# Token rows fetched from memory for all pairs of experts but the first, and two experts, not four, combined on the chip

## The chip, the cores and the metric

One core of a Trainium2 chip runs the whole program. The metric is the device time of one execution in microseconds, less is better. The kernel before took 1516.45 us in the median of three runs (1516.04 to 1519.44).

## What is computed

Two layers of a small diffusion trunk over 384 tokens of width 1024 (128 context tokens and 256 sample tokens, three tiles of 128). Layer 0 mixes by differential attention, layer 1 by retention; behind each mixer stands a mixture of experts (MoE), which is what matters here. Everything is float32.

```python
def group_moe(h, w_router, router_bias, w_gate, w_up, w_down):
    t = h.reshape(B * N, D)
    s = jax.nn.sigmoid((t @ w_router).astype(F32))
    ...            # the best of 4 groups, in it the best 2 of 4 experts
    w = w / jnp.sum(w, axis=-1, keepdims=True)
    gates = jnp.sum(jax.nn.one_hot(idx, N_EXPERTS, dtype=F32) * w[..., None], axis=1)

    def expert(y, p):
        wg, wu, wd, ge = p
        a = jax.nn.silu(t @ wg) * (t @ wu) * ge[:, None].astype(t.dtype)
        return y + a @ wd, None
```

16 experts, each with a gate and an up matrix of 1024 x 512 and a down matrix of 512 x 1024. A token uses two of them, so an expert has 48 tokens on average.

## The kernel before

The program is one instruction stream for each engine, written out by hand and tied by semaphores. PE does all matmuls, SP issues all loads of weights, ACT and DVE empty PSUM, POOL (GpSimd) issues indirect DMAs. `plan_jobs` numbers the PSUM banks' jobs in PE's order, `plan_units` the weights' loads.

**The MoE stage** (`experts(l)`, once a layer) turns the normalised activations into token rows `htok` (three tiles of 128 tokens x 1024), in two halves of 512 columns (L924, L1726). The router runs on DVE meanwhile. Then the experts come in pairs (q = 0 to 7, x = 0 or 1, e = 2q + x). For a block of 64 slots of each expert:

1. `gather` (L938, matmul L943): `htok` times a one-hot selection `sel` gives the two experts' tokens, features on partitions, in PSUM banks 2 and 3: 8 feature tiles x 3 token tiles = 24 matmuls a pair (48 instructions, since a float32 matmul is two). ACT copies them to `xs` (L1389), which is double-buffered.
2. gate and up matmuls (L1052, L1053), side by side in two halves of the array, 8 steps of 2 instructions each.
3. SiLU on ACT (L1418), times up on DVE (L1910), four transposes on PE (L1066), a copy by ACT (L1421), the down matmuls (L1083, L1084), a copy to `ysb` by DVE (L1916).

The gather of pair q + 1 stands in the work of pair q: for x = 0 bank 2, for x = 1 bank 3, three feature tiles between the gate matmuls and the wait for the product (L1062), the fourth between L1066 and the down matmuls (L1078). Tokens over 64 of an expert go through blocks of 32 in a loop of its own (`overflow`); in this run's data these are experts 5 and 6 of layer 0 and 4 to 7 of layer 1.

**The results.** `LAST` is 12. Experts 0 to 11 store their rows in HBM (`scratch`, traced as expert_rows, L1430). When expert 11's are stored, POOL reads two rows a token back with six indirect DMAs (L2053); ACT and DVE weigh and add them to `ytok` at the end of expert 13's iteration (L1439, L1920). Experts 12 to 15 are combined on the chip: the slot weights are turned (L1074), `combine` (L1017) multiplies the output by them, DVE adds the result to the residual xT (L1842, or L1583 for expert 15, the last). `side_plan` puts the combines of expert e - 1 in pairs behind odd gate steps of expert e, and the turning of `ytok` (L1032) behind L1074 of expert 14 and even steps of expert 15.

**The weights.** A unit is one 2 MB matrix. Nine places hold them (six in `ring`, three in pieces of other tiles, free only for experts 0 to 11). SP reloads a place when PE has passed L1066 (gate, up) or the down matmuls of the expert before in that place (L594); gate and up of expert 14 and 15 thus wait for L1066 of expert 12 and 13. The rows of expert e wait on ACT, POOL's read-back behind all stores.

Of the kernel before, what the change touches and what calls it, by code (L numbers as in the profile page):

```python
# [16 lines left out]
P = 128  # L17
D = 1024
# [16 lines left out]
LAST = NE - EPG  # L35


def side_plan():

    pair = lambda e, i: [("comb", e, i, 4), ("comb", e, i + 4, 7)]  # L40
    turn = lambda i: [("turn", None, i, 2), ("turn", None, i + 1, 3)]
# [16 lines left out]
WHOLE = 3 * LAST  # L58
# [5 lines left out]
def shape_constants():  # L64

    def angles(width):
# [13 lines left out]
        "first16": np.broadcast_to(np.arange(NE, 0, -1, dtype=np.float32), (P, NE)),  # L80
        "row0": np.broadcast_to(np.arange(NE, dtype=np.float32) * BLK, (P, NE)),
# [152 lines left out]
def trunk_kernel(nc, ins, outs, scratch):  # L234
# [31 lines left out]
    with ctx:  # L266
# [115 lines left out]
        def roT(f):  # L382
# [3 lines left out]
        wm = carve({"htok": TT * D, "xs": 2 * D, "sel": TT * P, "sg": 2 * 512, "aT": 2 * 256,  # L386
                    "y": 2 * 512, "osel": TT * OVB, "ox": KT * OVB, "osg": QC, "oa": QC, "oaT": 2 * BLK, "oy": QC,
                    "yg": TT * D, "selw": TT * P, "wT": TOK, "late": 2 * TOK, "G": TT * EPG, "G2": TT * EPG, "notl": TT, "dg": D, "s": TT * NE, "selb": TT * NE, "pair": TT * NG * 6, "gs": TT * NG,
                    "gm": TT, "gw": TT * NG, "gx": TT, "ing": TT * NG, "pen": TT * NG, "mx": TT, "w": TT * NE,
# [4 lines left out]
        xs = wm["xs"].rearrange("p (n k s) -> p n k s", n=2, k=KT)  # L394
        sel = wm["sel"].rearrange("p (t x s) -> p t x s", t=TT, x=2)
        sg = wm["sg"].rearrange("p (x f) -> p x f", x=2)
# [59 lines left out]
        for l in range(DEPTH):  # L456
# [4 lines left out]
                "o_stored", "picked", "half", "ytok", "passed", "side", "side_added", "selw", "selT", "wT",  # L461
                "o_selT", "o_wT", "o_comb", "o_added")})
# [160 lines left out]
        def _(pe):  # L623
# [292 lines left out]
            def experts(l):  # L916
# [97 lines left out]
                def combine(e, kt, out):  # L1014

                    rows = slice(BLK * (kt // 4), BLK * (kt // 4) + BLK)
                    return mm(out, ysb[rows, e % 2, P * (kt % 4):P * (kt % 4) + P], wT[rows, :], start=True, stop=True)  # L1017

                def side_work(at):

                    for kind, e, kt, place, n, before_, _ in side.get(at, ()):
                        if before_:
                            pe.wait_ge(m["side_added"], before_)
                        if kind == "comb":
                            pe.wait_ge(m["y"], e + 3)
                            pe.wait_ge(m["wT"], e - LAST + 1)
                            last = combine(e, kt, psum[:, place, 0:TOK])
                        else:
                            pe.wait_ge(m["xs"], NE)
                            pe.wait_ge(m["ytok"], TT)  # L1030
                            for t in range(TT):
                                last = tr(psum[:, place, P * t:P * t + P], ytok[:, t, P * kt:P * kt + P], ident)  # L1032
                        last.then_inc(m["side"], 1)

                pe.wait_ge(m["sel"], 1)
                for half in range(2):
                    gather(half, range(4 * half, 4 * half + 4)).then_inc(m["gathered"], 1)
                emptied(pe, ("rank", l))
                pe.wait_ge(m["routed"], 1)
                for it in range(NE // 4):  # L1040
                    for par in range(2):
                        q = it * 2 + par
                        for x in range(2):
                            e = q * 2 + x
                            wg, wu = unit(e, 0), unit(e, 1)
                            for kt in range(KT):
# [4 lines left out]
                                xk = xs[:, par, kt, BLK * x:BLK * x + BLK]  # L1051
# [25 lines left out]
                            if more:  # L1077
                                gather(x, (4 * x + 3,)).then_inc(m["gathered"], 1)  # L1078
# [129 lines left out]
        def _(act):  # L1208
# [158 lines left out]
            def experts(l):  # L1367
# [43 lines left out]
                for it in range(NE // 4):  # L1411
                    for par in range(2):
                        q = it * 2 + par
                        for x in range(2):
# [10 lines left out]
                            if q + 1 < NE // 2:  # L1425
                                take_xs(q + 1, 1 - par, x)
# [664 lines left out]
```

## Time and profile before

| | |
|---|---|
| median of three runs | 1516.45 us |
| the profiled execution | 1517.39 us, its span 1515.6 us |
| PE busy | 1405.8 us, 93% |
| DVE, ACT, POOL busy | 464.1, 281.0, 46.5 us |
| gate and up matmuls (L1052, L1053), with a ring place | 177.1 us each, x384, 605 ns |
| gathers (L943) | 107.0 us, x768, 292 ns |
| copies to xs by ACT (L1389) | 19.1 us, x32, 597 ns |
| chain that ended last | PE 86%; DVE 5%; DMA 3% |
| HBM read | 324.96 MB, 226 GB/s over the span |

The span is divided into 40 slices on the page, each digit a share in tenths; MoE stages are slices 9 to 16 and 31 to 39. A row of the timeline has the start, the length, the engine, line and operation, what it writes and reads, how many were merged, and in brackets the engine's idle time before it with what ended it.

### The profile page before, as it was taken

What the parts mean: (1) busy time and instruction counts of PE and PEld (TensorE: products, weight loads), DVE (VectorE), ACT (ScalarE), POOL (GpSimd) and SP (SyncE); (2) the same over time, 40 slices, a digit from 0 to 9 for tenths busy, and PEclk for the clock granted to TensorE, in tenths of its full rate; (3) what the DMA queues carried; (4) which work ended last, traced back from release to release, by engine and by line L of the source; (5) the groups of instructions that cost most, each with busy time, mean ns of one, the idle gap of its engine ahead of it and who ended that gap; (6) DMA issues with size and microseconds to landing.
All of it is one profiled execution on the core that took longest, in us unless ns stands there. A gap on an engine that the chain in (4) does not pass through costs nothing.

```text
span 1515.6 us, 17269 instructions
## 1 busy us (share of the span) xinstructions
PE 1405.8 (93%) x6556; PEld 721.1 (48%) x6556; DVE 464.1 (31%) x1360; ACT 281.0 (19%) x580; POOL 46.5 (3%) x63
## 2 busy tenths in 40 slices
PE   6999999989999998899999999996898998899887
PEld 2456465655444443344544545543555544444333
DVE  3156266342111135420611603405113211111354
ACT  2144245211101011310211202112101100001112
POOL 1001200000000010000100100000000000000100
PEclk9999999989999998999999999998899999999988
DMA  9877678748999999622233332234114897589951
GB/s 355 295 278 257 186 267 298 267 168 304 397 396 353 398 378 337 211 102 77 99 111 106 116 111 82 85 111 139 55 56 167 301 396 290 214 314 397 361 193 43
DMA packets 162100, 343.75 MB, mean 227 GB/s; under 512 B 5801, under 2 KB 23426, under 8 KB 161986
## 3 DMA queue, kind: packets, MB, share of 16 engines
q1 hardware_dynamic: 150320, 319.19, 57.5%
q0 software_dynamic: 2944, 9.65, 2.4%
q10 hardware_dynamic: 8722, 13.32, 2.4%
q8 instruction: 80, 1.31, 0.4%
q14 instruction: 34, 0.28, 0.1%
HBM read 324.96 MB, written 17.17 MB: 226 GB/s over the span
## 4 chain that ended last, share of the span: by engine, by line
PE 86%; DVE 5%; DMA 3%; ACT 2%; issue 2%; SPq 2%; DVEq 0%; ACTq 0%
PE psum L765 19%; PE psum L1052 14%; PE psum L758 11%; PE psum L1083 8%; PE psum L943 7%; PE psum L1176 6%; PE psum L894 3%; PE psum L1161 3%; PE psum L660 2%; PE psum L1017 2%; PE psum L988 2%; DMA ring<-in_da_w_qkv 1%; SPq L562 1%; DMA ring<-in_w_ada 1%; PE psum L1000 1%
## 5 line engine op out<-in xcount | busy, mean ns | idle before, releaser
L765 PE MATMUL psum<-ring,hT 128*128 128x512 f32 x672 | 289.4, 592 | 0.0
L765 PEld LDWEIGHTS psum<-ring,hT 128*128 128x128 f32 x672 | 127.7, 190 | 159.0 <-issue 157.8
L758 PE MATMUL psum<-hT,ring 128*128 128x384 f32 x512 | 172.9, 496 | 6.8 <-DMA ring<-in_da_w_qkv 3.8
L1053 PE MATMUL psum<-ring,work 128*64 128x512 f32 x384 | 177.1, 605 | 0.0
L1052 PE MATMUL psum<-ring,work 128*64 128x512 f32 x384 | 177.1, 605 | 0.0
L758 PEld LDWEIGHTS psum<-hT,ring 128*128 128x128 f32 x512 | 98.6, 194 | 75.7 <-issue 7.7
L943 PE MATMUL psum<-work 128*128 128x128 f32 x768 | 107.0, 292 | 11.9 <-issue 9.9
L943 PEld LDWEIGHTS psum<-work 128*128 128x128 f32 x768 | 95.8, 201 | 34.2 <-issue 30.4
L1052 PEld LDWEIGHTS psum<-ring,work 128*64 128x64 f32 x384 | 51.0, 138 | 106.8 <-issue 106.5
L1083 PE MATMUL psum<-ring,work 128*64 128x512 f32 x192 | 92.7, 628 | 1.6 <-issue 1.5
L1084 PE MATMUL psum<-ring,work 128*64 128x512 f32 x192 | 92.8, 629 | 0.0
L1916 DVE COPY work<-psum 128x512 f32<-128x512 f32 x32 | 22.1, 691 | 196.2 <-PE psum L1084 196.2
L1418 ACT ACTIVATE work<-psum 64x512 f32<-64x512 f32 x32 | 18.8, 588 | 338.9 <-PE psum L1053 338.9
L1910 DVE TENSOR_TENSOR work<-work,psum 64x512 f32<-64x512 f32 x32 | 22.1, 690 | 161.2 <-ACT work L1418 161.0
L1583 DVE SCALAR_TENSOR_TENSOR xT<-psum,mod,xT 128x128 f32<-128x128 f32 x64 | 22.5, 410 | 115.3 <-PE psum L1176 83.7
L1842 DVE SCALAR_TENSOR_TENSOR xT<-psum,mod,xT 128x128 f32<-128x128 f32 (+1 forms) x128 | 44.4, 410 | 29.3 <-PE psum L1017 25.4
L1961 DVE TENSOR_SCALAR work<-psum,work 128x256 f32<-128x256 f32 x4 | 1.9, 484 | 167.1 <-PE psum L1127 167.1
L660 PE MATMUL psum<-ring,cond 128*32 128x512 f32 x384 | 49.1, 634 | 2.2 <-DMA ring<-in_w_ada 2.1
L1053 PEld LDWEIGHTS psum<-ring,work 128*64 128x64 f32 x384 | 51.1, 138 | 0.0
L1083 PEld LDWEIGHTS psum<-ring,work 128*64 128x64 f32 x192 | 25.6, 144 | 49.5 <-issue 47.4
L1176 PE MATMUL psum<-sq,ring 128*128 128x384 f32 x128 | 45.4, 510 | 0.9 <-ACT hT L1448 0.9
L1176 PE MATMUL psum<-hT,ring 128*128 128x384 f32 x128 | 42.6, 486 | 0.0
(324 smaller groups left out, 1664.0 us busy)
## 6 DMA issues: line engine op xcount, KB each, us to landing
ring<-in_w_ada SPq DMA_DIRECT2D x24, 2048.0 KB, 12.7
ring<-in_moe_w_gate SPq DMA_DIRECT2D x24, 2048.0 KB, 13.1
ring<-in_moe_w_up SPq DMA_DIRECT2D x24, 2048.0 KB, 17.6
ring<-in_moe_w_down SPq DMA_DIRECT2D x24, 2048.0 KB, 18.8
ring<-in_da_w_qkv SPq DMA_DIRECT2D x6, 2048.0 KB, 15.7
sq<-in_moe_w_gate SPq DMA_DIRECT2D x8, 1536.0 KB, 12.4
hT<-in_moe_w_up SPq DMA_DIRECT2D x8, 1536.0 KB, 14.9
work<-in_moe_w_down SPq DMA_DIRECT2D x24, 512.0 KB, 11.0
```

Source lines behind the costliest of these rows:

```text
L660: last = mm(b[32 * j:32 * j + 32, :], cond[:, kt, :], w[:, kt, :], start=kt < 4, stop=kt >= 4)
L758: last = mm(b[:, 0:TOK], w[:, kt, col:col + P], hT[:, kt, :], start=kt == 0, stop=kt == KT - 1)
L765: last = mm(b, hT[:, kt, P * t:P * t + P], w[:, kt, :], start=kt == 0, stop=kt == KT - 1)
L894: last = mm(b[:, 0:TOK], w[:, h, P * (ft % 4):P * (ft % 4) + P], oT[:, h, :], start=h == 0, stop=h == HEADS - 1)
L943: last = mm(out, htok[:, t, P * kt:P * kt + P], sel[:, t].rearrange("p x s -> p (x s)"), start=t == 0, stop=t == TT - 1)
L1052: mm(psum[0:BLK, x, :], xk, wg[kt], start=kt == 0, stop=kt == KT - 1)
L1053: last = mm(psum[BLK:P, x, :], xk, wu[kt], start=kt == 0, stop=kt == KT - 1)
L1083: mm(psum[0:BLK, 5 + x, :], eaT[:, x, k, :], wd[k][:, 0:512], start=k == 0, stop=k == 3)
L1084: last = mm(psum[BLK:P, 5 + x, :], eaT[:, x, k, :], wd[k][:, 512:D], start=k == 0, stop=k == 3)
L1161: last = mm(b, a, v, start=n == 0, stop=n == len(terms) - 1)
L1176: last = mm(b[:, 0:TOK], w[:, k, P * (ft % 2):P * (ft % 2) + P], roT(k), start=k == 0, stop=k == 15)
L1842: last = V.scalar_tensor_tensor(out=xT[:, kt, a:z], in0=src[:, a:z], scalar=mod[:, l, 40 + kt, c:c + 1], in1=xT[:, kt, a:z], op0=ALU.mult, ...
```

## The change

- `LAST` becomes 14: experts 12 and 13 store their rows too, the read-back starts when expert 13's are stored, and only 14 and 15 are combined on the chip.
- ACT stores `htok` in HBM (`token_rows`), one DMA for each half.
- For pairs 1 to 7, PE multiplies `sel` by a column of token numbers (`list_tokens`, 3 matmuls of one column), DVE writes the 128 numbers as integers (`token_list`), POOL fetches the 128 rows of 4 KB into `xrow` with one indirect DMA (`row_loads`), PE turns them (`turn_rows`, 4 transposes for each expert of the pair). Pair 0 is gathered as before. `xs` and `xrow` have one buffer each; ACT copies both halves in the second expert's iteration.
- The fourth part of the gather between L1066 and the down matmuls is gone.
- The turning of `ytok` in the middle is gone: at the end PE adds it to the combines of expert 15 in the same banks, as matmuls with the identity.

```diff
-LAST = NE - EPG
+LAST = NE - 2
+ONCHIP = NE - LAST
...
-    plan[(NE - 2, "T")] = turn(0)
-    for i in range(3):
-        plan[(NE - 1, 2 * i)] = turn(2 * i + 2)
...
# PE
+                def list_tokens(q):
+                    pe.wait_ge(m["sel"], q + 1)
+                    if q > 1:
+                        pe.wait_ge(m["listed"], q - 1)
+                    chosen = sel_second if q == 1 else sel
+                    for t in range(TT):
+                        last = mm(psum[:, 4, 0:1], chosen[:, t].rearrange("p x s -> p (x s)"),
+                                  table(base_sb, base_at, "token")[:, t:t + 1], start=t == 0, stop=t == TT - 1)
+                    last.then_inc(m["ids"], 1)
+                def turn_rows(q, half):
+                    pe.wait_ge(m["rows"], 16 * q)
+                    pe.wait_ge(m["xs"], 2 * q)
+                    for kt in range(4 * half, 4 * half + 4):
+                        last = tr(psum[:, 2 + half, P * (kt % 4):P * (kt % 4) + P], xrow[:, P * kt:P * kt + P], ident)
+                    last.then_inc(m["gathered"], 1)
                 pe.wait_ge(m["sel"], 1)
-                for half in range(2):
-                    gather(half, range(4 * half, 4 * half + 4)).then_inc(m["gathered"], 1)
+                gather(0, range(4)).then_inc(m["gathered"], 1)
                 emptied(pe, ("rank", l))
+                list_tokens(1)
+                gather(1, range(4, KT)).then_inc(m["gathered"], 1)
...
                             overflow(e, wg, wu, hint)
                             more = q + 1 < NE // 2
+                            if x == 0 and q + 2 < NE // 2:
+                                list_tokens(q + 2)
                             if more:
-                                pe.wait_ge(m["sel"], q + 2)
-                                pe.wait_ge(m["xs"], q * 2 + x + 1)
-                                gather(x, range(4 * x, 4 * x + 3))
+                                turn_rows(q + 1, x)
                             pe.wait_ge(m["gated"], e + 1)
...
-                            if more:
-                                gather(x, (4 * x + 3,)).then_inc(m["gathered"], 1)
...
                 for ft in range(KT):
-                    b = open_job(("y", l, ft))
-                    done(combine(NE - 1, ft, b[:, 0:TOK]))
+                    combine(NE - 1, ft, early(("y", l, ft))[:, 0:TOK], stop=False)
+                pe.wait_ge(m["ytok"], TT)
+                for ft in range(KT):
+                    b = early(("y", l, ft))
+                    for t in range(TT):
+                        last = mm(b[:, P * t:P * t + P], ytok[:, t, P * ft:P * ft + P], ident, start=False, stop=t == TT - 1)
+                    open_job(("y", l, ft))
+                    done(last)
# ACT
+                for half in range(2):
+                    emptied(act, ("htok", l, TT * half + TT - 1))
+                    act.dma_start(token_rows_d.rearrange("(t p) d -> p t d", p=P)[:, :, 512 * half:512 * half + 512],
+                                  htok[:, :, 512 * half:512 * half + 512]).then_inc(m["kept"], 16)
...
-                            if q + 1 < NE // 2:
-                                take_xs(q + 1, 1 - par, x)
+                            if x and q + 1 < NE // 2:
+                                take_xs(q + 1, 0)
+                                take_xs(q + 1, 1)
# DVE
+                def token_list(q):
+                    dve.wait_ge(m["ids"], q)
+                    V.tensor_copy(ids[:, q:q + 1], psum[:, 4, 0:1]).then_inc(m["listed"], 1)
                 select(0)
+                select(1)
...
                             overflow(e, lo, hint)
+                            if x == 0 and q + 2 < NE // 2:
+                                token_list(q + 2)
# POOL, ahead of pick_rows(l)
+            def row_loads(l):
+                m = M[l]
+                pool.wait_ge(m["kept"], 32)
+                for q in range(1, NE // 2):
+                    pool.wait_ge(m["listed"], q)
+                    if q > 1:
+                        pool.wait_ge(m["gathered"], 2 * q)
+                    pool.indirect_dma_start(out=xrow, out_offset=None, in_=token_rows_d,
+                                            in_offset=bass.IndirectOffsetOnAxis(ap=ids[:, q:q + 1], axis=0)).then_inc(m["rows"], 16)
```

## Rows read from the trace of the kernel before

**Rows 1.** Busy time by stretch: length, engines, PE clock, DMA share, GB/s.

```profile
348.20:538.20 190.00, 182.78 (x1163) 86.91 (x1164) 26.62 (x55) 21.35 (x40) 0.00 (x0) 1.00 0.98 370
538.20:617.50 79.30, 71.44 (x342) 28.27 (x338) 38.81 (x104) 10.15 (x17) 5.72 (x6) 0.94 0.82 304
1182.50:1406.10 223.60, 206.49 (x1535) 99.58 (x1536) 33.77 (x76) 22.39 (x43) 0.00 (x0) 1.00 0.86 321
1406.10:1493.80 87.70, 75.02 (x342) 30.39 (x338) 38.87 (x104) 12.48 (x25) 5.67 (x6) 0.90 0.59 221
...
370.00:442.00 72.00, 69.45 (x467) 33.50 (x467) 10.47 (x22) 7.63 (x15) 0.00 (x0) 1.00 1.04 398
454.00:466.00 12.00, 9.66 (x106) 6.06 (x100) 1.57 (x5) 1.25 (x3) 0.00 (x0) 1.00 0.73 257
```

**Rows 2.** Timeline of expert 0 in layer 0, a plain one.

```profile
348.20 0.64 PE L1052 MATMUL psum<-ring,work 128*64 128x512 f32 x1
...
354.69 0.59 PE L1052 MATMUL psum<-ring,work 128*64 128x512 f32 x1
...
355.22 2.27 PE L943 MATMUL psum<-work 128*128 128x128 f32 x18
...
355.96 0.69 DVE L1910 TENSOR_TENSOR work<-work,psum 64x512 f32<-64x512 f32 x1 [6.46 <-ACT work L1418]
...
357.43 0.46 PE L1066 MATMUL psum<-base_sb,work 64*128 64x64 f32 x4
...
358.68 0.64 PE L1083 MATMUL psum<-ring,work 128*64 128x512 f32 x1
...
362.17 0.59 PE L1052 MATMUL psum<-ring,work 128*64 128x512 f32 x1
```

**Rows 3.** Timeline of experts 14 and 15 in layer 0, around L1066.

```profile
589.52 0.69 DVE L1910 TENSOR_TENSOR work<-work,psum 64x512 f32<-64x512 f32 x1
...
590.36 0.43 PE L1066 MATMUL psum<-base_sb,work 64*128 64x64 f32 x4 [2.36 <-DVE work L1910]
...
613.08 0.43 PE L1066 MATMUL psum<-base_sb,work 64*128 64x64 f32 x4 [2.36 <-DVE work L1910]
...
614.00 0.13 PEld L1083 LDWEIGHTS psum<-ring,work 128*64 128x64 f32 x1 [0.25 <-issue]
```

**Rows 4.** Timeline: transposes of 128x128, and matmuls of one column.

```profile
597.94 0.88 PE L1032 MATMUL psum<-base_sb,sq 128*128 128x128 f32 x6
...
1507.30 0.73 PE L705 MATMUL psum<-base_sb,ssp 128*128 128x1 f32 x6
```

**Rows 5.** Landing times: line L2053, line L1430, then loads issued in 1417 to 1418.

```profile
DMA to landing us min/median/max: 4.6/10.0/12.6
...
DMA to landing us min/median/max: 5.2/5.8/6.9
...
ring<-in_moe_w_up SPq DMA_DIRECT2D x1, 2048.0 KB, 21.9
```

**Rows 6.** Timeline of experts 13 and 14 in layer 0.

```profile
552.37 0.59 PE L1052 MATMUL psum<-ring,work 128*64 128x512 f32 x1
...
566.08 0.46 PE L1066 MATMUL psum<-base_sb,work 64*128 64x64 f32 x4
...
592.90 1.06 PE L1083 MATMUL psum<-ring,work 128*64 128x512 f32 x1
```

**Rows 7.** Loads of expert 15's up unit: issued in 566 to 568, 1440 to 1441.

```profile
ring<-in_moe_w_up SPq DMA_DIRECT2D x1, 2048.0 KB, 19.4
...
ring<-in_moe_w_up SPq DMA_DIRECT2D x1, 2048.0 KB, 15.8
```

**Rows 8.** Timeline: ytok in layer 0, the tail of layer 1.

```profile
572.04 3.68 DVE L1920 SCALAR_TENSOR_TENSOR sq<-hT,work,sq 128x1024 f32<-128x1024 f32 x3
...
1494.83 4.25 PE L1017 MATMUL psum<-work 64*128 64x384 f32 x16 [0.79 <-DVE work L1916]
1495.85 5.29 DVE L1583 SCALAR_TENSOR_TENSOR xT<-psum,mod,xT 128x128 f32<-128x128 f32 x16 [1.07 <-PE psum L1017]
```

More of the change, by code:

```diff
@@ L80, in shape_constants @@
         "first16": np.broadcast_to(np.arange(NE, 0, -1, dtype=np.float32), (P, NE)),
+        "token": (P * np.arange(TT)[None, :] + part[:, None]).astype(np.float32),
         "row0": np.broadcast_to(np.arange(NE, dtype=np.float32) * BLK, (P, NE)),
@@ L393, in trunk_kernel @@
         htok = wm["htok"].rearrange("p (t d) -> p t d", t=TT)
-        xs = wm["xs"].rearrange("p (n k s) -> p n k s", n=2, k=KT)
+        xs = wm["xs"].rearrange("p (k s) -> p k s", k=KT)
         sel = wm["sel"].rearrange("p (t x s) -> p t x s", t=TT, x=2)
+        second = wm["at"]["osg"]
+        sel_second = work[:, second:second + TT * P].rearrange("p (t x s) -> p t x s", t=TT, x=2)
+        ids = wm["ids"].bitcast(mybir.dt.uint32)
+        xrow = wm["xrow"]
         sg = wm["sg"].rearrange("p (x f) -> p x f", x=2)
@@ L461, in trunk_kernel @@
                 "o_stored", "picked", "half", "ytok", "passed", "side", "side_added", "selw", "selT", "wT",
+                "kept", "ids", "listed", "rows",
                 "o_selT", "o_wT", "o_comb", "o_added")})
@@ L1012, in overflow, with combine @@
                                 pe.sem_inc(m["o_comb"], 2)
-                def combine(e, kt, out):
+                def combine(e, kt, out, stop=True):
                     rows = slice(BLK * (kt // 4), BLK * (kt // 4) + BLK)
-                    return mm(out, ysb[rows, e % 2, P * (kt % 4):P * (kt % 4) + P], wT[rows, :], start=True, stop=True)
+                    return mm(out, ysb[rows, e % 2, P * (kt % 4):P * (kt % 4) + P], wT[rows, :], start=True, stop=stop)
                 def side_work(at):
@@ L1023, in side_work @@
                             pe.wait_ge(m["side_added"], before_)
[L1024 to L1032, printed above, removed]
-                        last.then_inc(m["side"], 1)
+                        pe.wait_ge(m["y"], e + 3)
+                        pe.wait_ge(m["wT"], e - LAST + 1)
+                        last = combine(e, kt, psum[:, place, 0:TOK])
+                        last.then_inc(m["side"], 1)
+                def list_tokens(q):
[13 more added lines that the diff above has]
+                    last.then_inc(m["gathered"], 1)
                 pe.wait_ge(m["sel"], 1)
-                for half in range(2):
-                    gather(half, range(4 * half, 4 * half + 4)).then_inc(m["gathered"], 1)
+                gather(0, range(4)).then_inc(m["gathered"], 1)
                 emptied(pe, ("rank", l))
+                list_tokens(1)
+                gather(1, range(4, KT)).then_inc(m["gathered"], 1)
                 pe.wait_ge(m["routed"], 1)
@@ L1385, in experts, with take_xs @@
                 act.sem_inc(m["o_stored"], 64)
-                def take_xs(pair, par, half):
+                def take_xs(pair, half):
                     act.wait_ge(m["gathered"], pair * 2 + half + 1)
-                    A(xs[:, par, 4 * half:4 * half + 4, :].rearrange("p k s -> p (k s)"), psum[:, 2 + half, :], ACT.Copy).then_inc(m["xs"], 1)
+                    A(xs[:, 4 * half:4 * half + 4, :].rearrange("p k s -> p (k s)"), psum[:, 2 + half, :], ACT.Copy).then_inc(m["xs"], 1)
                 def overflow(e, hint):
@@ L2087 @@
     scratch = nc.dram_tensor("expert_rows", ((LAST + MAXOV) * BLK, D), mybir.dt.float32, kind="Internal").ap()
-    trunk_kernel(nc, ins, outs, scratch)
+    token_rows_d = nc.dram_tensor("token_rows", (TOK, D), mybir.dt.float32, kind="Internal").ap()
+    trunk_kernel(nc, ins, outs, scratch, token_rows_d)
     r = run_bass_kernel_spmd(nc, [arrays], core_ids=[0])
```

41 lines of the change are left out of this document (23 added, 18 removed).

## The prediction

> **What bounds the kernel now.** I read the page's 40 slices first, then the stretches of the two mixture-of-experts (MoE) stages, then the timeline of single experts. The change touches only these two stages: experts 0 to 11 of layer 0 run from 348.2 to 538.2, 12 to 15 to 617.5; layer 1 has 1182.5 to 1406.1 and then to 1493.8. In the first stretch PE is busy 183 of 190 us and the 16 DMA engines work at a share of 0.98; in long parts of it they are at 1.04 and 398 GB/s, which is as full as the trace ever shows them [rows 1]. So two resources are close to their ends: PE takes 13.9 us for a plain expert, and its 6.3 MB of weights (three units of 2.097 MB) take about 16.1 us at 390 GB/s. The transfers keep up only because nine units are loaded ahead, and because experts with a second block and the last four experts run slowly. In layer 1 there is more of that slowness, and the DMA share is 0.86, then 0.59 [rows 1]. Layer 0 is thus nearly bound by the weights, layer 1 is bound by PE and its waits.
>
> **Part 1, the gathers become transposes (7 of 8 pairs in each layer).** In a plain expert the first gate matmul is at 348.20 and that of the next expert at 362.17. The last gate matmul starts at 354.69 and is through at 355.12; 18 gather instructions fill 355.22 to 357.43, where the transposes of the gated block (L1066) start; the other 6 of the 24 follow, and the down matmuls start at 358.68 [rows 2]. But these gathers were cover. SiLU and the product (L1910) run beside them; the product starts at 355.96. Where no gather stands, L1066 starts 0.84 us after the product's start (589.52 to 590.36), so here it could start at 356.80 and not at 357.43: about 0.65 us are won. Between L1066 and the down matmuls the bare distance is 0.92 us (613.08 to 614.00) against 1.25 with six gathers [rows 2, 3]: 0.3 us. Instead of about 3.1 us of PE work an expert thus gives back about 0.95 us. The new work fits under the same cover: four transposes are about 0.5 us (six last 0.88, starts 0.12 apart), the token list's six one-column matmuls 0.7 us [rows 4]; together 1.2 of the 1.65 us between the last gate matmul and L1066. An expert goes from 13.9 to 13.0 us on PE. With a second block the cover isn't needed, and about 1.7 us are won. At the start of a stage one list and one more selection (DVE) cost 0.7 us once. Halves 0 and 1 of the next pair are now both copied by ACT behind the second expert's L1066: 1.2 us under 3.4 us of down matmuls, so free; without them, xs would be late by these 1.2 us.
>
> **Part 2, where the rows come from.** ACT issues two stores of 0.79 MB, POOL seven fetches of 128 rows (0.52 MB), one a pair. Queued behind each on POOL are the later fetches and then the read-back of expert rows. A fetch starts when the pair before is turned, and PE waits for it after the next expert's gate matmuls: 0.5 us of turning less, that is 1.1 + 0.95 + 3.45 + 6.9 + 0.7 = 13 us later. The nearest rows are the read-backs of the same size, 4.6 us at least and 12.6 at most (six in a row, the last ones behind the first), and the stores of 128 KB in a full stage, 5.2 to 6.9 us [rows 5]. I take 6 us plus 1 us of POOL, by the first of a row; both ends fit into 13, so the fetch is hidden. The price is in bytes. For the first fetch: the rows are written by about 339, the store of half 1 lands some 8 to 9 us later by these rows, the fetch at 353 to 355, and it's wanted at 355.8. I take 0, with 0 to 3 us for each layer.
>
> As for the arbitration, the row shows that the quickest read-back landed after 4.6 us, while a load of 2 MB issued beside the read-backs at 1417.6 took 21.9 us [rows 5]. The Trainium skill (DMA: Bandwidth & Descriptors, "Queues, rings and completion order") says that every DMA engine takes turns between the queues that have work. By that the fetch doesn't stand behind the weights, and the trace agrees; standing behind them it would be the last rival below.
>
> **Part 3, the last four experts.** Removed per layer: the combines of experts 12 and 13, the slot weights and their three transposes, the read-back rows' turning in the middle, and the stalls around them. In layer 0 24.3 us lie between the L1066 of experts 13 and 14 (566.08, 590.36), because DVE first finishes the read-back rows, PE waits for it, the last time 2.36 us, and the clock falls [rows 3, 6]. Now 12, 13 and 14 take 13.0 us each on PE. Expert 15 keeps eight combines, like 13 before: 552.37 to 566.08 less 0.5 us of cover and then 4.4 us, together 17.6 us [rows 6]. The sum is 56.6 us against 79.3 and 87.7. On PE alone the stages would get shorter by 35 us (12 from the gathers, 0.7 lost, 23 here) and 45 us (14 and 31). That isn't the gain, as the weights don't come that fast.
>
> **Part 4, the weights as the new bound.** Expert 15's up unit is the last that gates PE. In layer 0 it is issued at 567.1 and lands 19.4 us later, at 586.5 [rows 7]. The queue has been nearly full since 357. What comes on top before that point is six fetches (3.1 MB) and the rows of experts 12 and 13 (0.5 MB): 3.7 MB, or 9.4 us at 390 GB/s. Off goes the hole at 454 to 466 (share 0.73, 3.6 us [rows 1]), since PE frees slots earlier. So it lands at about 592.3. Behind it stand 10.9 us of gate and up with combines, 2 us for a half clock after the wait (a down matmul lasted 1.06 instead of 0.59 us after such a wait [rows 6]), 2.3 to L1066, 0.95, and 3.45 of down: 19.6 us. The stage ends at 611.9 instead of 617.5, 5.6 us earlier.
>
> In layer 1 it is issued at 1440.7 and lands at 1456.5 [rows 7]. Now expert 7 frees its slot about 10 us earlier, at 1335 (eight experts: 4 at 0.95 and 4 at 1.7, less 0.7). From there to that unit 17 units, six experts' rows, two or three fetches and the 3.1 MB of read-backs have to pass, 42 MB, so 108 us and 2 of latency: 1445 to 1446. PE would be there at about 1435 and waits 10 us. With the same 19.6 us the stage ends at 1465.4, 28.4 us earlier.
>
> **Part 5, the new tail.** The read-back rows are now added after expert 15. The combines start 0.75 us after the copy of y starts and last 3.9 us to the last issue. Beside them DVE makes ytok (3.68 us behind the 0.69 us copy), and ACT's halves lie under the down matmuls. Then come 48 instructions at 0.12 us, 5.6 us, and a last residual of 0.7 us: 11.1 us from the copy. Before it is 7.1 us (16 residuals end at 1501.1) [rows 8]. Cost: 4.0 us a layer, 8 in all. The read-backs themselves start about 6.5 us after expert 13 and need 19; experts 14 and 15 with their wait last over 40 us, so they are hidden.
>
> **Sum.** -5.6 - 28.4 + 8 = -26 us, and I keep -25.5 for what remains of the sequencer's stalls in layer 1. The profiled execution took 1517.39 us (span 1515.6) and would take 1492; it is 0.06% over the median of 1516.45, so the forecast of the median is 1491 us.
>
> **The rivals.**
>
> Rival A, the transfers give more. With 397 GB/s held throughout (the full stretches show 398) the unit of expert 15 lands some 6 us earlier in layer 0 and 3 in layer 1: 1481 us. For it speaks [rows 1], against it that read-backs and weights together came to 389.
>
> Rival B, a slower clock. Every expert now has two short waits on PE, some 1.1 and 0.5 us. After three of the four waits of 2.36 us the granted clock was down at the next down matmuls. If it falls to 1.2 GHz in every expert for about four matmul pairs, each costs 1.7 us, and a plain expert 14.7 us, 0.8 more than before. Layer 0 stays on its weights (-5), layer 1 gets slower by 7 (-21): 1498 to 1500 us. Against it: the waits are half as long, and transposes stand in them. The Trainium skill (TensorE: Matmul & The Clock Gate, "What's actually happening") has idle time as what throttles and sustained work as what releases; [rows 6] agree for the long waits, no row shows the short ones.
>
> Rival C, on the other side: the fetches come late. If a fetch stands behind queued weights like a load of 2 MB, it lands after 22 us and not 7, and PE idles 9 us at each of six pairs in each layer. That takes 54 us where PE alone would have gained 35 and 45: +19, +9 and the tail's 8, so 1552 us. It decides from a landing time of about 19 us (6 us late a pair, where 36 eats the gain). Against it are [rows 5].
>
> Rival D, it does nothing to the time: with one DMA resource full in both layers and clock and first fetch each at their bad end (3 us each, 2 more in each wait), the gain of layer 1 shrinks to the tail's price: 1514 us. Little speaks for all of this together.
>
> **How the numbers follow.** Forecast 0.60 (1484 to 1500 for it alone), A 0.12, B 0.13, C 0.09, D 0.06. The range goes from below A (bandwidth and stalls both kind, 1476) to above B (first fetch late, 1508) and leaves C, D and a bit of A out. Within 0.2%, 1513.4 to 1519.5, is what a measurement of this kernel can't tell from no change; that is D for the most part, 0.05. Faster: 0.60 + 0.12 + 0.13 less a bad end of B = 0.83. Slower 0.12.
>
> **What would show it right or wrong.** Plain experts of 13.0 us, with L1066 about 1.65 us after the gate matmuls. PE waits for DMA on the ring before the gate matmuls of experts 12 to 15, longest (about 10 us) before 15. DMA share over 1.0 up to about 590 in layer 0. The layer-0 stage shorter by 1 to 3 us with its tail, layer 1 by some 24. POOL's fetches landing in 5 to 8 us. Wrong would be: waits for xrow before the turning, a granted clock of 0.5 inside plain experts, or ytok as the last releaser at the tail by several us.

## The result, and the profile after

The changed kernel takes 1506.04 us (median of 4 runs, 1504.49 to 1507.36), the kernel before 1516.24 beside it (1515.92 to 1519.44). The ratio is 0.9921, 95% interval 0.9904 to 0.9937: 10 us faster, 0.8%. 25.5 us were forecast. The profiled execution took 1504.49 us, its span is 1502.6; that is 13.0 less than the span of before, 1515.6.

The first rows are busy time by stretch of the changed kernel: experts 0 to 11 and 12 to 15 of layer 0, the same of layer 1, and the middle of layer 0 once more (columns as in [rows 1]).

```profile
347.00:529.60 182.60, 161.41 (x959) 69.45 (x959) 29.96 (x76) 20.17 (x40) 5.91 (x7) 0.98 1.02 388
529.60:611.70 82.10, 59.67 (x238) 21.38 (x237) 15.18 (x40) 8.96 (x15) 5.62 (x6) 0.81 0.93 349
1180.80:1402.70 221.90, 188.85 (x1329) 82.55 (x1330) 36.91 (x96) 21.30 (x43) 6.61 (x7) 0.96 0.88 334
1402.70:1475.50 72.80, 53.77 (x240) 19.81 (x236) 15.21 (x40) 11.23 (x23) 5.63 (x6) 0.91 0.79 303
400.00:587.00 187.00, 152.59 (x886) 64.30 (x883) 28.53 (x68) 16.83 (x35) 9.37 (x10) 0.93 1.04 397
```

Beside [rows 1] the four stretches went from 190.0, 79.3, 223.6 and 87.7 us to 182.6, 82.1, 221.9 and 72.8. The last four experts of layer 0 got longer, though PE works 12 us less in them (59.7 instead of 71.4), and the first twelve of layer 1 are hardly shorter, though PE works 17.6 us less in them. The last row holds the reason for layer 0: 187 us at a DMA share of 1.04 and 397 GB/s, as full as the fullest row of [rows 1] and without its hole.

Next, what PE waited for in each stage of the changed kernel (us in total, times, longest), layer 0 and then layer 1.

```profile
PE psum L1069 <- DMA ring<-in_moe_w_up: 13.1, 2, 6.6
PE psum L1098 <- issue: 11.5, 14, 2.7
PE psum L1083 <- DVE work L1946: 8.8, 12, 1.5
PE psum L1083 <- issue: 4.9, 1, 4.9
...
PE psum L1098 <- issue: 13.9, 14, 2.4
PE psum L1083 <- DVE work L1946: 10.0, 11, 2.3
PE psum L1069 <- DMA ring<-in_moe_w_up: 9.4, 1, 9.4
...
PE psum L1069 <- issue: 2.9, 1, 2.9
...
PE psum L1048 <- DMA work<-token_rows,work: 2.0, 1, 2.0
```

In both layers the gate matmuls (L1069) now wait for weights. The 11.5 and 13.9 us ahead of the down matmuls (L1098) are waits of about 0.5 us, one in each plain expert up to 13, and six of 1.8 to 2.7 us; those stand in the experts with a second block. This is expert 5 of layer 0, from the end of its second block on (timeline: start, duration, what it does, in brackets the idle time before and what ended it):

```profile
429.23 0.66 PE L1048 MATMUL psum<-base_sb,work 128*128 128x128 f32 x4
...
429.82 0.46 PE L1083 MATMUL psum<-base_sb,work 64*128 64x64 f32 x4
...
430.10 1.95 ACTq L1430 DMA_DIRECT2D expert_rows<-work  x4
...
432.27 0.38 ACT L1446 ACTIVATE work<-psum 128x256 f32<-128x256 f32 x1 [6.20 <-issue]
...
432.75 1.09 PE L1098 MATMUL psum<-work 128*64 128x512 f32 x1 [2.47 <-issue]
...
433.63 1.06 PE L1098 MATMUL psum<-work 128*64 128x512 f32 x1
```

The turned block is ready at about 430.3, but ACT copies it at 432.27, because its queue first issues the four stores of the second block's rows (1.95 us). PE idles 2.47 us, and then its matmuls last 1.06 to 1.09 us, not 0.59: half clock. Before, the same four issues lay under 18 gathers and the transposes behind them:

```profile
435.09 2.28 PE L943 MATMUL psum<-work 128*128 128x128 f32 x18
...
435.96 1.86 ACTq L1405 DMA_DIRECT2D expert_rows<-work  x4
...
437.30 0.46 PE L1066 MATMUL psum<-base_sb,work 64*128 64x64 f32 x4
...
438.03 0.38 ACT L1421 ACTIVATE work<-psum 128x256 f32<-128x256 f32 x1 [6.09 <-PE psum L1066]
...
438.55 0.64 PE L1083 MATMUL psum<-work 128*64 128x512 f32 x1
```

Last, expert 0 of layer 1 in the changed kernel, where the first fetch comes late, and the landing times of the fetches (L2086) and of the stores of the rows (L1406):

```profile
1190.60 1.11 PE L1048 MATMUL psum<-base_sb,work 128*128 128x128 f32 x4 [1.99 <-DMA work<-token_rows,work]
...
1192.86 1.08 PE L1098 MATMUL psum<-ring,work 128*64 128x512 f32 x1 [0.52 <-issue]
...
DMA to landing us min/median/max: 7.0/8.4/9.2
...
DMA to landing us min/median/max: 7.6/8.0/9.1
```

PE waits 1.99 us ahead of the turning (L1048), then the down matmuls run at half clock, and the expert takes 17.5 us instead of 13.0.

### The profile page after: what moved, and what is told of

Read it like the earlier page. It is cut to its first block, busy times and chain, and to the rows that moved or that the text cites. A ratio compares the mean times of both kernels' runs of the same rounds, so it can differ in the third digit from the quotient of the medians.

```text
span 1502.6 us, 16129 instructions
## 1 busy us (share of the span) xinstructions
PE 1341.8 (89%) x6052; PEld 680.2 (45%) x6052; DVE 428.1 (28%) x1256; ACT 276.4 (18%) x576; POOL 59.6 (4%) x77
## 4 chain that ended last, share of the span: by engine, by line
PE 75%; DMA 11%; DVE 4%; SPq 4%; issue 3%; ACT 3%; DVEq 0%; ACTq 0%; POOLq 0%
PE psum L768 19%; PE psum L761 11%; PE psum L1069 11%; PE psum L1098 6%; PE psum L1197 6%; DMA ring<-in_moe_w_up 5%; PE psum L897 3%; PE psum L1182 3%; SPq L597 2%; PE psum L663 2%; PE psum L991 2%; DMA ring<-in_da_w_qkv 1%; SPq L565 1%; DMA token_rows<-work 1%; DMA work<-token_rows,work 1%
## 5 line engine op out<-in xcount | busy, mean ns | idle before, releaser
L1069 PE MATMUL psum<-ring,work 128*64 128x512 f32 x384 | 178.6, 617 | 25.5 <-DMA ring<-in_moe_w_up 22.5
L1070 PE MATMUL psum<-ring,work 128*64 128x512 f32 x384 | 178.8, 618 | 0.0
L1069 PEld LDWEIGHTS psum<-ring,work 128*64 128x64 f32 x384 | 53.2, 142 | 132.2 <-issue 131.9
L1098 PE MATMUL psum<-ring,work 128*64 128x512 f32 x192 | 96.9, 652 | 17.7 <-issue 17.6
L1099 PE MATMUL psum<-ring,work 128*64 128x512 f32 x192 | 97.5, 656 | 0.0
L1098 PEld LDWEIGHTS psum<-ring,work 128*64 128x64 f32 x192 | 26.6, 149 | 65.0 <-issue 65.0
L1070 PEld LDWEIGHTS psum<-ring,work 128*64 128x64 f32 x384 | 53.1, 142 | 0.0
L663 PE MATMUL psum<-ring,cond 128*32 128x512 f32 x384 | 46.0, 598 | 2.8 <-DMA ring<-in_w_ada 2.7
L1197 PE MATMUL psum<-sq,ring 128*128 128x384 f32 x128 | 45.2, 509 | 0.9 <-ACT hT L1474 0.9
L1069 PE MATMUL psum<-sq,work 128*64 128x512 f32 x96 | 42.5, 592 | 0.0
L1070 PE MATMUL psum<-hT,work 128*64 128x512 f32 x96 | 42.5, 592 | 0.0
L897 PE MATMUL psum<-sq,ring 128*128 128x384 f32 x128 | 42.1, 488 | 0.0
## 6 DMA issues: line engine op xcount, KB each, us to landing
ring<-in_w_ada SPq DMA_DIRECT2D x24, 2048.0 KB, 12.6
ring<-in_moe_w_up SPq DMA_DIRECT2D x24, 2048.0 KB, 19.6
```

Of the source, the lines that this page charges most:

```text
L663: last = mm(b[32 * j:32 * j + 32, :], cond[:, kt, :], w[:, kt, :], start=kt < 4, stop=kt >= 4)
L897: last = mm(b[:, 0:TOK], w[:, h, P * (ft % 4):P * (ft % 4) + P], oT[:, h, :], start=h == 0, stop=h == HEADS - 1)
L1069: mm(psum[0:BLK, x, :], xk, wg[kt], start=kt == 0, stop=kt == KT - 1)
L1070: last = mm(psum[BLK:P, x, :], xk, wu[kt], start=kt == 0, stop=kt == KT - 1)
L1098: mm(psum[0:BLK, 5 + x, :], eaT[:, x, k, :], wd[k][:, 0:512], start=k == 0, stop=k == 3)
L1099: last = mm(psum[BLK:P, 5 + x, :], eaT[:, x, k, :], wd[k][:, 512:D], start=k == 0, stop=k == 3)
```

## The experiments

Theory 1: the missing gain is PE time lost in the experts with a second block and in expert 0 of layer 1, so that slots come free late, and above that the bytes ahead of expert 15's up unit. Theory 2: the transfers alone set both stages, whatever PE does. The table gives for every kernel the four stretches of the profiled execution in us (from first gate matmul to first gate matmul, the last stretch of a layer to the end of expert 15's down matmuls), the median, and its ratio to the kernel before with the interval.

| kernel | L0, 0-11 | L0, 12-15 | L1, 0-11 | L1, 12-15 | us | ratio |
|---|---|---|---|---|---|---|
| before | 190.0 | 79.3 | 223.6 | 87.7 | 1516.2 | 1 |
| changed | 182.6 | 82.1 | 221.9 | 72.8 | 1506.0 | 0.9921 (0.9904-0.9937) |
| k1_one_store | 185.2 | 81.5 | 210.4 | 74.8 | 1498.1 | 0.9873 (0.9853-0.9892) |
| k2_late_turn | 184.1 | 80.0 | 217.6 | 74.7 | 1502.2 | 0.9907 (0.9890-0.9923) |
| k3_no_fetch | 181.9 | 79.0 | 222.1 | 68.0 | 1493.4 | 0.9838 (0.9817-0.9860) |
| k6_both | 184.5 | 80.1 | 212.0 | 78.3 | 1497.5 | 0.9863 (0.9842-0.9884) |
| k4_gather_last14 | 190.8 | 63.2 | 223.5 | 61.7 | 1483.1 | 0.9770 (0.9755-0.9786) |
| k5_fetch_last12 | 184.2 | 92.3 | 217.4 | 81.6 | 1512.4 | 0.9971 (0.9960-0.9982) |
| k8_held | 184.5 | 75.4 | 217.0 | 65.0 | 1491.1 | 0.9831 (0.9813-0.9850) |
| k7_one_store_held | 185.1 | 75.7 | 213.2 | 66.8 | 1483.9 | 0.9780 (0.9767-0.9792) |
| k9_gather_store_held | 188.9 | 61.7 | 225.4 | 63.2 | 1481.1 | 0.9748 (0.9724-0.9771) |
| k10_no_fetch_one_store | 178.4 | 79.0 | 212.3 | 68.3 | 1483.1 | 0.9767 (0.9744-0.9790) |
| k11_all_three | 184.7 | 76.0 | 212.1 | 65.9 | 1483.9 | 0.9772 (0.9749-0.9795) |

The ratio of k1, k2, k3 and k6 is to one set of runs of the kernel before (median 1516.6), that of k4, k5, k7 and k8 to another (1516.9), that of k9, k10 and k11 to a third (1518.2). So a difference of 2 us between medians of different sets tells nothing. A profile is one execution, and in it down matmuls run at half clock in some experts and not in others: a stretch differs by 1.7 us for each such expert.

**One store in place of four.**

```diff
-for j in range(4):
-    act.dma_start(scratch[ds(o * OVB + LAST * BLK, OVB), QC * j:QC * j + QC],
-                  oy[OVB * j:OVB * j + OVB, :]).then_inc(m["o_stored"], 16)
+act.dma_start(scratch[ds(o * OVB + LAST * BLK, OVB), :].rearrange("s (j c) -> j s c", j=4),
+              oy).then_inc(m["o_stored"], 16)
```

The waits that count these transfers are adapted.

> The changed kernel, but the rows of each second block go to memory with one transfer that ACT issues, not with four. Theory 1 (the missing gain of layer 1 sits in the experts with a second block: the gathers used to cover ACT's four transfer issues, 1.95 us, and now the down matmuls wait for ACT's copy and then run at half clock): in these experts the wait ahead of the down matmuls falls from 2.3 to 3.2 us to about 1.2, the down matmuls from about 5 to 3.5 us, so each of the six takes some 22.5 to 24 us (the two-block one 34) instead of 24.3 to 26.9; expert 15's up unit is issued 8 to 11 us earlier in layer 1 and the whole kernel takes 1494 to 1498 us instead of 1506. Theory 2 (the transfers of layer 1 are full and set its end, whatever PE does): the experts get quicker, the wait for the weights ahead of experts 14 and 15 gets longer by the same time, and the kernel stays at 1504 to 1506 us. In layer 0, where both theories have the weights as the bound, 0 to 2 us.

Measured 1498.1 us, 8 less, at the slow end of theory 1's range. The same place in its timeline:

```profile
432.02 1.16 ACTq L1429 DMA_DIRECT2D expert_rows<-work  x1
...
433.39 0.38 ACT L1445 ACTIVATE work<-psum 128x256 f32<-128x256 f32 x1 [5.39 <-issue]
...
433.87 0.61 PE L1098 MATMUL psum<-work 128*64 128x512 f32 x1 [1.67 <-issue]
```

One issue takes 1.16 us where four took 1.95, PE idles 1.67 us, not 2.47, and the clock holds (0.61). The six experts take 23.5, 25.1, 25.1, 34.3, 23.7 and 23.4 us, where the changed kernel had 25.7, 26.9, 26.3, 37.2, 24.3 and 25.9: 11.2 us less, 7.1 of it in layer 1. Two of the six still fell to half clock (25.1 us). The single profile flatters layer 1 by 4.5 us, since its expert 0 happened not to wait for the fetch. Theory 1 holds in layer 1, and theory 2 fails, as the bytes are the same. In layer 0 nothing is gained: the stage is 2 us longer in this profile, and PE waits 10.4 us for the weights ahead of expert 15, where the changed kernel has 6.6.

**The first fetched pair turned later.**

```diff
-if more:
+if more and q:
     turn_rows(q + 1, x)
+if x and q == 0:
+    turn_rows(1, 0)
+    turn_rows(1, 1)
```

> The changed kernel, but both halves of the pair of experts 2 and 3 are turned behind expert 1's gate matmuls, and none behind expert 0's, so the first fetch has 13 us more. Theory 1: expert 0 of layer 1 goes from 17.5 back to 13.0 us (2.0 us of waiting for the fetch, 2.5 us of half clock behind it); expert 1 gains at most 0.3 us for its four more transposes; the kernel takes 1502 to 1503.5 us instead of 1506. Theory 2 (transfers set the end of layer 1): 1505.5 to 1506.5 us, with a wait for the weights that is 4 us longer ahead of experts 14 and 15.

Measured 1502.2 us, 3.8 less by the medians, in theory 1's range. The mechanism fits only in part: expert 0 of layer 1 takes 14.7 us, not the 13.0 of theory 1. The wait for the fetch is gone, but its down matmuls still ran at half clock (5.15 us to the next expert's start, in place of 3.46), in layer 0 too.

**Six fetches left out.**

```diff
 pool.wait_ge(m["listed"], q)
 if q > 1:
-    pool.wait_ge(m["gathered"], 2 * q)
+    continue
```

PE then waits for the first fetch alone.

> The changed kernel with six of the seven fetches of each layer left out: experts 4 to 15 work on the rows that the first fetch brought, so their part of the result isn't the reference's. It takes 3.1 MB a layer off the queues and any wait for these fetches. The forecast priced these bytes at about 8 us ahead of expert 15's up unit in layer 0, so its stage ends 6 to 8 us earlier, and in layer 1, where PE's own time decides when that unit is issued, 1 to 3 us: 1495 to 1499 us. If bandwidth alone sets the end of both stages (theory 2) both give 8 us: about 1490 us. If the fetches cost nothing (the queues have room for them) it stays within 1504 to 1506 us.

Measured 1493.4 us, 12.6 less, more than the forecast's price (1495 to 1499 us) and less than theory 2's (about 1490). Its profiled execution was the slowest of its four (1498.35 us), so the split by stage is only rough: -3.8 in layer 0, -4.6 in layer 1, where expert 15 alone lost 3.7 us, for the most part to half clock (23.3 us, not 19.6). In layer 0 the 3.1 MB are 7.8 us at 397 GB/s; by an estimate 2.0 of them went back because the queue then ran empty for a while, with a share of 0.88 in this stretch,

```profile
453.00:466.00 13.00, 9.78 (x116) 5.33 (x110) 1.72 (x6) 0.76 (x2) 0.00 (x0) 1.00 0.88 314
```

Another 1.9 us, by which expert 0 was longer at half clock (14.9 us, not 13.0), would make up the rest; that this held back the transfers by as much is not shown.

**Both repairs of PE's waits.** The two edits above in one kernel.

> The changed kernel with the one transfer for the rows of a second block and the late turning of the first fetched pair together. Theory 1: both gains add in layer 1, as both bring the issue of expert 15's up unit forward, less what the queues then can't carry (expert 15's unit would wait behind others for 2 to 4 us): 1491 to 1495 us, near the 1491 us that were forecast. Theory 2: 1504 to 1506 us.

Measured 1497.5 us, outside both ranges and not told apart from k1_one_store. The gains don't add: the first twelve experts of layer 1 are 9.9 us shorter than in the changed kernel, but the last four 5.5 us longer. Of these 5.5 us 3.7 are expert 15 itself (23.3 us, not 19.6, with its down matmuls at half clock), in a profiled execution 4 us above the median. Theory 1's sum was too simple here.

**The second half of the change alone.** To the kernel before, gathers kept:

```diff
-LAST = NE - EPG
+LAST = NE - 2
+ONCHIP = NE - LAST
```

with the change's parts that follow from it: the side plan without turning, the mask of two experts, and the tail with the identity.

> The second half of the change alone: the kernel before with its gathers kept, but only experts 14 and 15 combined on the chip and the read-back rows added by the identity in the tail. No rows are stored or fetched (3.7 MB a layer less than in the changed kernel), and the experts with a second block keep the gathers that cover ACT's four transfer issues. Theory 1 (the fetches' bytes and the lost cover took most of what the transposes give): nearly all of the gain is here. Layer 1: experts 12 to 14 at 13.9 us, the weights for 15 about 1449 to 1453, its stage ends at about 1471 instead of 1493.8; layer 0: up unit at 584 to 587, stage end 604 to 611; two tails of 4 us; together 1490 to 1498 us, faster than the changed kernel's 1506. Rival (the transposes in place of the gathers carry the gain, as PE bounds both layers): 1504 to 1512 us.

Measured 1483.1 us: 34 us faster than before, 23 faster than the whole change, beyond what was expected. Busy time by stretch, same four as above:

```profile
348.90:539.70 190.80, 182.84 (x1163) 86.90 (x1164) 26.63 (x55) 21.35 (x40) 0.00 (x0) 1.00 0.98 370
539.70:602.90 63.20, 59.36 (x280) 23.61 (x276) 15.68 (x41) 9.17 (x15) 5.73 (x6) 0.92 1.02 383
1171.00:1394.50 223.50, 206.29 (x1533) 99.47 (x1534) 33.79 (x76) 22.37 (x43) 0.00 (x0) 1.00 0.87 323
1394.50:1456.20 61.70, 56.67 (x280) 22.90 (x276) 15.70 (x41) 11.50 (x23) 5.67 (x6) 0.97 0.81 309
```

The first twelve experts are as before, and the last four are 16.1 and 26.0 us shorter. Ahead of no expert does PE wait for weights. With experts of 13.9 us the transfers just keep up; with 13.0 us and the fetches' bytes on top they don't.

**The first half of the change alone.** The changed kernel with the old split:

```diff
-LAST = NE - 2
+LAST = NE - EPG
```

and the turning of the read-back rows back in the side plan, the combines of expert 15 closing the tail by themselves.

> The first half of the change alone: rows kept in memory, fetched and turned for seven of eight pairs, but the last four experts combined on the chip and the read-back rows turned beside them, as before. Theory 1: eight plain experts a layer give 0.95 us each on PE, second-block experts give nothing or lose 1 to 2 us each, the first fetch of layer 1 costs up to 4.5 us, and in layer 0 the 3.1 MB of fetches delay expert 15's up unit by up to 5 us: 1512 to 1519 us, no gain that can be told. Rival (the forecast's own terms, 0.95 and 1.7 us for each expert with nothing against them in layer 1): layer 1 gives 12 us, layer 0 loses up to 5: 1504 to 1510 us.

Measured 1512.4 us, 4.5 less than before (0.3%), at the good end of theory 1's range and outside the rival's. It wins 5.8 and 6.2 us in the first twelve experts of the two layers and 6.1 in the last four of layer 1, and loses 13.0 in the last four of layer 0, where PE waits 10.9 us for weights ahead of expert 13. Halves of 34 and 4.5 us together give 10: the first half takes away much of what the second half brings.

**The read-backs held until the last up unit has landed.**

```diff
+unit_wait(pool, ("moe", l, 3 * (NE - 1) + 1))
 settle(pool, l)
 idx = wm["idx"].bitcast(mybir.dt.uint32).rearrange("p (c t) -> p c t", c=2)
```

> The changed kernel, but POOL issues the six read-backs of expert rows (3.1 MB) only when expert 15's up unit has landed, not 8 to 12 us before. Theory 1 (the bytes that lie in the queues ahead of that unit set when the last expert starts; the read-backs' 3.1 MB are 7.8 us of it at 397 GB/s): expert 15's gates start at 579 to 582 us instead of 586.7 in layer 0 and at 1448 to 1450 instead of 1456.1 in layer 1, and the rows are still in time for the tail (they need 14 us, the tail comes 25 us later): 1490 to 1496 us. Rival (a 2 MB unit needs its 15 to 30 us whatever else is queued, or the rows then come too late for the tail): the start of expert 15 moves by less than 2 us or the tail waits for ytok by what was won: 1504 to 1508 us.

Measured 1491.1 us, 15 less. The start of expert 15 in layer 1, first in the changed kernel, then in this one:

```profile
1425.27 8.21 SPq L597 DMA_DIRECT2D ring<-in_moe_w_up  x1
...
1437.10 0.94 POOL L2102 DMA_INDIRECT work<-expert_rows,work  x1 [37.98 <-DMA expert_rows<-work]
...
1456.06 1.09 PE L1069 MATMUL psum<-ring,work 128*64 128x512 f32 x1 [9.41 <-DMA ring<-in_moe_w_up]
```

```profile
1419.47 8.50 SPq L597 DMA_DIRECT2D ring<-in_moe_w_up  x1
...
1442.88 0.61 PE L1069 MATMUL psum<-ring,work 128*64 128x512 f32 x1 [0.83 <-DMA ring<-in_moe_w_up]
...
1443.54 0.94 POOL L2103 DMA_INDIRECT work<-expert_rows,work  x1 [51.61 <-DMA ring<-in_moe_w_up]
```

From its issue to expert 15's start the up unit took 30.8 us, though the read-backs were issued 12 us after it; now it takes 23.4, 7.4 less, and the last four experts take 65.0 us instead of 72.8. The 3.1 MB alone are 7.8 us at 397 GB/s. (In both, 8.2 to 8.5 us of this are the issue itself on SP; in the kernel before the issue of this unit took 0.5.) The tail is no longer (27.2 us from the end of the stage to that of the span, 27.1 in the changed kernel). In layer 0 the last four win 6.7 us. Another 4.5 us in layer 1 are luck of this profile: its expert 0 didn't wait for the fetch. Expert 15 starts at 584.8 in layer 0, later than expected, and in layer 1 at 1442.9, earlier.

The Trainium skill (DMA: Bandwidth & Descriptors, "Queues, rings and completion order") has every DMA engine take turns between the queues that have work. These rows agree: what was issued later on another queue went ahead of part of the queued weights. The prediction used the rule for the fetches. It also counted the read-backs' bytes ahead of the unit (they are in the 42 MB of part 4), but didn't ask whether they have to be there: nothing needs them before the tail.

**One store and held read-backs.** Both edits in one kernel.

> The kernel with one transfer for the rows of a second block (1498 us) and the held read-backs together. Theory 1: the two act on different terms, when slots come free and what is queued ahead of the last unit, so they add: 1484 to 1490 us. Rival as for the held read-backs alone: 1496 to 1500 us.

Measured 1483.9 us, at theory 1's lower end: the two gains add (1506.0 less 8.0 and 14.9 is 1483.1).

**Both edits on the kernel with gathers.**

> The kernel with gathers and the last two experts on the chip (1483.1 us), with the one transfer for the rows of a second block and the held read-backs added. Theory 1: in that kernel PE no longer waits for weights (0.0 and 0.2 us ahead of expert 15) and the gathers cover ACT's four transfer issues, so neither edit finds anything to remove: 1480 to 1484 us. Rival (both edits are good by themselves, in any kernel, as they were worth 8 and 15 us in the changed one): 1465 to 1475 us.

Measured 1481.1 us, against 1483.1 with intervals that overlap. There was little for them to remove, as theory 1 says: each edit pays mostly for something that the first half of the change brought. Not quite nothing, though: the six experts with a second block take 2.3 us less together than in k4_gather_last14 (157.1 us, not 159.4), which a difference of 2 us in the medians neither shows nor excludes. It is the lowest median of all kernels here, but not told apart from k4_gather_last14.

**No fetches and one store.**

> The changed kernel without six of the seven fetches a layer (experts 4 to 15 work on the rows of the first fetch, so their part of the result isn't the reference's) and with the one transfer for the rows of a second block. It prices what the fetches' bytes and the lost cover take together. Theory 1: the bytes (12.6 us by the run without them) and the cover (8.0 us) are the two things that turn the 34 us of the kernel with gathers into 10, so this is about as quick as that one or a little quicker, as its plain experts take 13.0 us and not 13.9: 1478 to 1487 us. Rival (the two overlap, since both act on the same wait for the last weights): 1491 to 1494 us.

Measured 1483.1 us, in theory 1's range: bytes (12.6 us) and cover (8.0) add to 20.6, and 23 were measured from the changed kernel. They are the whole distance to the kernel with gathers. This kernel still has the plain experts of 13.0 us, but PE waits 10.0 and 8.8 us for weights ahead of expert 15 in the two layers, where the kernel with gathers and 13.9 us waits for none, and the totals are the same: what the transposes give back on PE became waiting.

**All three repairs.**

> The changed kernel with all three repairs: one transfer for the rows of a second block, the late turning of the first fetched pair, and the held read-backs. Theory 1: against the kernel with the first and the third (1483.9 us) expert 0 of layer 1 gets back 2 to 3 us of its 17.5: 1480 to 1483 us. Rival (after the other two repairs the weights set the end, so an earlier PE only waits longer): 1483 to 1486 us.

Measured 1483.9 us, the rival's range. Expert 0 of layer 1 took 14.7 us where k7_one_store_held had 17.5, but expert 15's gates start 260.4 us after the stage's start and there 260.7. The rival's number came, but its reason isn't shown by this pair of profiles: expert 6 lost 1.7 us to half clock here and not there, expert 14 once more, and PE waits for no weights ahead of expert 15 (1.8 us there). Ahead of expert 14 PE idles 4.4 and 4.5 us, with no releaser shown. What sets the end of layer 1 then stays open.

## Why the prediction was right and wrong

Right: direction, range (1476 to 1508) and much of the mechanism. Plain experts take 13.0 us, L1083 comes 1.69 us after the gate matmuls, PE waits 9.41 us for weights ahead of expert 15 in layer 1 (10 forecast), fetches are hidden from pair 2 on. The wait fits by luck: the forecast's own terms bring PE to expert 15 at 1431 (1406.1 less 13.7, and three experts of 13.0), not 1435, so 14 us before the weights. PE was there at 1446.7 and the weights at 1456.1, 15 and 11 us later than the terms say. The range held only near its slow end. The new tail costs 4.1 us in layer 0 (from the end of the stage to the start of layer 1's, 565.0 to 569.1 us) and 5.3 at the end, 9.4 together for 8 forecast; the 48 additions with the identity last 5.62 us.

```profile
1476.40 4.24 PE L1020 MATMUL psum<-work 64*128 64x384 f32 x16 [0.79 <-DVE work L1954]
1480.57 5.62 PE L1110 MATMUL psum<-base_sb,sq 128*128 128x128 f32 x48
1481.62 5.37 DVE L1609 SCALAR_TENSOR_TENSOR xT<-psum,mod,xT 128x128 f32<-128x128 f32 x16 [1.56 <-PE psum L1110]
```

Wrong: the size, by the term of layer 1. Its stage became 16.6 us shorter, not 28.4. Part 4 took expert 7's slot as free at 1335, with "4 at 0.95 and 4 at 1.7, less 0.7". That is 13.7 us for the first twelve experts with the four plain ones after it; they gave 1.7. The parts: the four experts with a second block went from 109.3 to 113.8 us, 4.5 more where 6.8 less were forecast (11.3 us); expert 0 took 4.5 more than the forecast 13.0; stalls of before that were not in the forecast went away (3.0 us, experts 3 and 9), and the 0.7 us at the start don't fall into this stretch. From expert 12 on the forecast was met: 73.0 us by its terms (1465.4 less 1392.4), 72.8 measured.

The step that failed is the sentence of part 1, "With a second block the cover isn't needed, and about 1.7 us are won". It looked for the cover of SiLU and the product, which a second block does give, and not at ACT's queue: four issues of about 0.5 us each stand there ahead of the copy that PE needs next. The row at 435.96 has these issues: they stand under the gathers, and without gathers they stand on the path. The six experts won 0.9 to 1.6 us each before L1066, lost 0.4 to 1.7 between L1066 and the down matmuls, and five of them another 1.4 to 1.7, as these then ran at half clock. The run with one store shows the issues' part by the edit of that line alone: 8.0 us by the medians. It leaves 1 to 1.7 us of waiting in each of these experts.

Part 2 took 7 us from issue to landing of a fetch and 8 to 9 for the store. Measured in layer 1: 8.4 for the first fetch and 9.1 for the store, so the fetch landed at 1190.6, 2 us late. The prediction had this as a bound (0 to 3 us) but priced the wait and not the 2.5 us of half clock behind it. It isn't in every profile: of the kernels that turn the pair early, k1_one_store, k5_fetch_last12 and k8_held don't have the wait, and k10_no_fetch_one_store has it without the half clock.

Layer 0 came out near its term (4.6 us for 5.6) by two errors that cancel. The up unit was there at 586.7, not 592.3: the transfers ran at 397 GB/s, not 390, which was rival A's case and worth about 4 us of the 5.6 by an estimate (90 MB at either rate). And expert 15 took 25.0 us, not 19.6, with a stall of 4.92 us ahead of L1083 and half clock behind it.

Of the rivals, B happened in a form that it didn't describe: not in the plain experts 1 to 13 with their two short waits (all at full clock, 3.46 us of down matmuls), but after waits of about 2 us, and not after each of them (after 1.79 us ahead of L1098 in expert 6 of layer 1 the down matmuls took 3.46 us). C didn't happen; D's ingredients did, in part.

What the prediction missed most stands in none of its terms: the two halves of the change work against each other. It valued part 1 at 12 and 14 us of PE time and then said itself that the weights don't come that fast. Followed to its end, this asks what the first half is worth at all if PE is not the bound: by the runs 4.5 us alone, and less than nothing (23 us lost) beside the second half. Of these 23 us the fetches' bytes are 12.6 and the issues 8.0, each by a run.

## What to carry to other kernels

When instructions go away, look at what every other engine and queue does during them, the issuing of DMAs too: on the path, four small issues can cost more than the matmuls that hid them. Where PE and the transfers are both nearly full, time taken from PE with bytes added to the queues is a poor exchange; try each half of a change alone. And a transfer that isn't needed until later should be issued later: here one from another queue wasn't put behind the weights that were already queued (fetches landed after 8.4 us in the median, while a 2 MB weight unit took 30.8).

## What was not expected of the hardware

The read-backs, issued 12 us after a weight unit, delayed it by 7.4 us, nearly the full time of their own bytes (7.8 us for 3.1 MB).

Expert 15 of layer 0 has a stall of PE ahead of L1083 for which the profile shows no releaser, 4.92 us in the changed kernel:

```profile
601.88 0.69 DVE L1946 TENSOR_TENSOR work<-work,psum 64x512 f32<-64x512 f32 x1
...
605.34 0.66 PE L1083 MATMUL psum<-base_sb,work 64*128 64x64 f32 x4 [4.92 <-issue]
```

The product that L1083 turns is ready at 602.57, so 2.8 us of the stall have no reason in the program. The distance from the gate matmuls to L1083 in this expert is 5.9 us in the changed kernel, 3.7 to 7.6 in the other variants that turn fetched rows and have two experts on the chip, and 3.3 to 3.4 with gathers or with four experts on the chip. In layer 1 it is 3.3 to 3.4 in every kernel. The DMA queues still carry work at that point in layer 0 (231 GB/s over 598 to 606 in the changed kernel, 368 in k7_one_store_held) and are empty in layer 1 (6 GB/s over 1466 to 1474).

The packets of the traces point at one thing. In all nine kernels with this stall in layer 0 a packet of 16 KB on the instruction queue (q8, here 602.70 to 603.77) ends 1.5 to 1.7 us before PE starts again; in the four kernels without the stall no packet ends then. So PE may be waiting for its next instructions, which come late through full queues. That is argued from the times alone; no run was made to tell it. The stall may also be a part of why holding the read-backs gave less in layer 0 than in layer 1: there it grew from 4.9 to 6.6 us.
